# Two chained transformer blocks on one core: one merged norm stage with the narrow products in it, attention with stationary values, decay rows by transposes

## The reference

```python
# first block: bidirectional gated delta net, 8 heads of 128, chunks; then a 16-expert MoE
gcum = jnp.cumsum(g, axis=-1)
diff = gcum[..., :, None] - gcum[..., None, :]
decay = jnp.where(incl, jnp.exp(jnp.where(incl, diff, 0.0)), 0.0)
...
return rmsnorm(h, final_g)
# second block, on that result x
hx = rms_norm(x, norm1) * (1 + sc1) + sh1          # 1024 latent rows
hc = rms_norm(ctx, norm1) * (1 + csc1) + csh1      # 256 context rows
zx, xbc_x, dt_x, qx, kx, vx = split_projection(hx @ w_in)   # widths 512, 1024, 16, 512, 128, 128
zc, xbc_c, dt_c, qc, kc, vc = split_projection(hc @ w_in)
... # depthwise convolution and silu on xbc, two state-space scans, times silu(z), norm
# windowed attention: 8 query heads, 2 key/value heads, head width 64
p = softmax_with_sink(jnp.concatenate([s_loc, s_ctx], axis=-1), sink)
o = einsum('bnhgqk,bnkhd->bnqhgd', p_loc, vw) + einsum('bnhgqk,bkhd->bnqhgd', p_ctx, v_ctx)
x = x + g1 * (concatenate([ssd_x, attn_x]) @ w_out)
# then a 32-expert MoE and a last norm
```

## Time and profile before

| | us |
|---|---|
| median of 3 runs | 4789.37 (4787.4 to 4795.4) |
| profiled execution: time | 4788.9 |
| profiled execution: span of the profile | 4786.9 |
| PE busy in the span | 4181.8 (87%) |
| DVE, ACT, POOL busy | 1566.7, 795.1, 403.6 |
| norm stages n3 and n4, to the first projection product | 2809.5 to 2926.8 |
| projection, main part | 2926.8 to 3173.3 |
| projection, narrow products | 3173.3 to 3248.3 |
| attention, first product to last copy | 3432.0 to 3637.6 |

### The profile page before, as it was taken

One profiled execution on the slowest core, in us unless ns is written; L12 is line 12 of the kernel. 1 busy time (PEld: TensorE's weight loads), 2 busy tenths in 40 slices (PEclk: granted clock), 3 DMA queues, 4 the chain that ended last, 5 costly groups with the idle time before them and its releaser, 6 DMA issues. The chain is left out here.

```text
span 4786.9 us, 43588 instructions
## 1 busy us (share of the span) xinstructions
PE 4181.8 (87%) x15052; PEld 2319.5 (48%) x15052; DVE 1566.7 (33%) x3340; ACT 795.1 (17%) x1787; POOL 403.6 (8%) x388
## 2 busy tenths in 40 slices
PE   6699999997959999999999945997798789999962
PEld 3466666665414444444444423456675344444421
DVE  4577777775350000000000034416743400000003
ACT  2233333332110000000000001101252110001001
POOL 0111111110000000000000000004300000000001
PEclk8899999998969999999999967998799899999986
DMA  6211111111469888888888822100102189999855
GB/s 260 50 33 36 35 38 35 39 26 30 179 269 359 307 308 309 307 310 305 309 309 311 311 93 92 28 9 5 68 1 110 51 319 335 334 335 335 305 206 215
DMA packets 434795, 875.48 MB, mean 183 GB/s; under 512 B 88722, under 2 KB 132578, under 8 KB 428506
## 3 DMA queue, kind: packets, MB, share of 16 engines
q1 hardware_dynamic: 408361, 785.27, 46.6%
q0 software_dynamic: 20320, 74.06, 4.6%
q10 hardware_dynamic: 5968, 14.29, 0.8%
HBM read 801.14 MB, written 72.43 MB: 182 GB/s over the span
## 5 line engine op out<-in xcount | busy, mean ns | idle before, releaser
L1823 PE MATMUL moe_gbank<-moe_ring,moe_xT 128*128 128x512 f32 x1536 | 679.7, 596 | 3.8 <-ACTq L1879 3.8
L1841 PE MATMUL moe_acc<-moe_ring,moe_hidT 128*128 128x512 f32 x1536 | 675.1, 592 | 1.8 <-DVEq L1938 1.1
L1823 PE MATMUL moe_ubank<-moe_ring,moe_xT 128*128 128x512 f32 x1536 | 675.1, 592 | 0.0
L1913 DVE TENSOR_TENSOR moe_hid<-moe_sg,moe_ubank 128x512 f32<-128x512 f32 x96 | 66.0, 688 | 1631.8 <-PE moe_ubank L1823 1631.8
L921 PE MATMUL gdn_pbank<-mix_xT,gdn_w 128*128 128x512 f32 (+1 forms) x1280 | 540.8, 556 | 2.6 <-PEq L815 2.6
L1823 PEld LDWEIGHTS moe_gbank<-moe_ring,moe_xT 128*128 128x128 f32 x1536 | 293.4, 191 | 373.6 <-issue 370.3
L1841 PEld LDWEIGHTS moe_acc<-moe_ring,moe_hidT 128*128 128x128 f32 x1536 | 288.2, 190 | 347.1 <-issue 347.1
L1823 PEld LDWEIGHTS moe_ubank<-moe_ring,moe_xT 128*128 128x128 f32 x1536 | 284.5, 190 | 322.4 <-issue 322.4
L1884 ACT ACTIVATE moe_sg<-moe_gbank 128x512 f32<-128x512 f32 x96 | 57.3, 597 | 1547.4 <-PE moe_gbank L1823 1547.4
L921 PEld LDWEIGHTS gdn_pbank<-mix_xT,gdn_w 128*128 128x128 f32 x1280 | 230.2, 195 | 161.2 <-issue 152.4
L2059 PE MATMUL proj_abank<-mix_yT,proj_wq 128*128 128x512 f32 x416 | 180.8, 592 | 0.6 <-PE proj_abank L2059 0.6
(11 more groups left out here) (520 smaller groups left out, 4940.0 us busy)
## 6 DMA issues: line engine op xcount, KB each, us to landing
moe_ring<-in_moe_w_gate SPq DMA_DIRECT2D x64, 2048.0 KB, 7.9
moe_ring<-in_moe_w_up SPq DMA_DIRECT2D x64, 2048.0 KB, 7.8
moe_ring<-in_moe_w_down SPq DMA_DIRECT2D x64, 2048.0 KB, 7.8
moe_ring<-in_w_gate SPq DMA_DIRECT2D x32, 2048.0 KB, 8.7
moe_ring<-in_w_up SPq DMA_DIRECT2D x32, 2048.0 KB, 9.4
moe_ring<-in_w_down SPq DMA_DIRECT2D x32, 2048.0 KB, 9.8
front_wt<-in_w_mod SPq DMA_DIRECT2D x24, 1024.0 KB, 13.9
route_wt<-in_w_ada SPq DMA_DIRECT2D x24, 1024.0 KB, 16.0
```

The lines of the kernel that those rows point to most:

```text
L1823: last = nc.tensor.matmul(bank[:], xT[:, k, :], w[:, k * 512:(k + 1) * 512], start=(k == 0), stop=(k == KD - 1))
L1841: last = nc.tensor.matmul(acc[j][:], hidT[:, k, :], w[:, k * D + j * 512:k * D + (j + 1) * 512], start=(f == 0 and k == 0), stop=(f == NF ...
L1913: nc.vector.tensor_tensor(hid[:], sg[:], ubank[:], ALU.mult).then_inc(u_free, 1)
```

## The change

1. `delta_net`: the decay rows' calls become transposes of the same broadcast column.
2. `n3` and `n4` become one stage `norms_and_narrow`. Its parameters for both kinds of rows are loaded ahead, ACT takes over the sums of squares, and the z, dt and v products are made there, one token tile behind the transposes. It uses four x buffers and three y buffers. The first two weight tiles of the projection and the convolution weights are loaded at its end.
3. `project` loses the narrow products, their loads and the first two weight loads; silu of z is one instruction at its end.
4. `attention`: the values are stationary (64 columns) and the probabilities move, two heads at once (256 columns). Even heads go to PSUM partitions 0 to 63, odd ones to 64 to 127 of the same bank. The reciprocals are spread over partitions by four small products, DVE copies them out and multiplies straight into `yT2`. `at`, its transposes and their copies are gone.

```diff
 # delta_net, fill
-  last = nc.tensor.matmul(b[:, q * P:(q + 1) * P], tab[:, n, C_, u:u + 1].broadcast_to([P, P]), ident, start=True, stop=True)
+  last = nc.tensor.transpose(b[:, q * P:(q + 1) * P], tab[:, n, C_, u:u + 1].broadcast_to([P, P]), ident)
 # attention, PE
-  for g in range(QPK):
-      for c in kt:
-          last = nc.tensor.matmul(obank[u % 2][:, g * HD:(g + 1) * HD], pT[:, c, g, :], vtok[:, vt, kv * HD:(kv + 1) * HD], ...)
-  last.then_inc(o_full, 1)
-  ... (after the last unit: transposes of at, per token tile)
+  for c in kt:
+      for odd in range(2):
+          last = nc.tensor.matmul(obank[u % 2][odd * HD:(odd + 1) * HD, 0:2 * P], vtok[:, vt, kv * HD:(kv + 1) * HD], pT[:, c, odd::2, :], ...)
+  last.then_inc(o_full, 1)
+  pe.wait_ge(rec_ready, u + 1)
+  for g in range(QPK):
+      j, odd = divmod(g, 2)
+      last = nc.tensor.matmul(obank[u % 2][odd * HD:(odd + 1) * HD, (2 + j) * P:(3 + j) * P], stats[u % RING][:, REC_, g:g + 1].broadcast_to([P, HD]), ident, start=True, stop=True)
+  last.then_inc(r_full, 1)
 # attention, DVE: for each unit reciprocals(u), maxima(u + 2), divide(u)
-  nc.vector.tensor_tensor(at[...], obank[...], stat[:, REC_, :]..., ALU.mult).then_inc(o_free, 1)
+  nc.vector.tensor_copy(rb[...], bank[:, 2 * P:4 * P])
+  dve.drain()
+  nc.vector.tensor_tensor(yT2[:, 4 + 2 * kv:6 + 2 * kv, n * P:(n + 1) * P], bank[:, 0:2 * P]..., rb[:], ALU.mult).then_inc(o_free, 1)
 # project
-  for t in range(NA): ... z and dt/v products, their copies out, wz and wv loads
-  nc.scalar.activation(z[:, t, :], b[:], ACT.Silu).then_inc(a_free, 1)
+  nc.scalar.activation(z[...all eight tiles...], z[...], ACT.Silu)
```

More of the change, by code:

```diff
@@ L1949, in softplus_steps, with project @@
     nc.vector.tensor_scalar(x, x, 0.0, None, ALU.max)
-def project(nc, xT, w_in, conv_w, conv_b, cst, ident, BC, Btok, xs, z, dtr, qT, kT, vtok):
+def project(nc, xT, w_in, cst, ident, BC, Btok, xs, z, qT, kT, cwr, wq):
     XT = 8
@@ L1959, in project @@
     with Stage(nc, "proj") as st:
-        cwr = st.sb("cwr", [(CONV + 1) * XT, P])
         cw = st.sb("cw", [P, (CONV + 1) * XT])
-        wq = [st.sb(f"wq{i}", [P, KD, P]) for i in range(2)]
-        wz = st.sb("wz", [P, KD, 512])
-        wv = st.sb("wv", [P, KD, 2 * SH + KVH * HD])
         raw = [st.sb(f"raw{i}", [P, PADTOK]) for i in range(2)]
@@ L2069, in _ @@
                         rotate(i - 1)
-                for t in range(NA):
-                    if t >= NC_T:
-                        b = a_bank()
-                        for k in range(KD):
-                            last = nc.tensor.matmul(b[:], x_cols(k, t * P, P), wz[:, k, :], start=(k == 0), stop=(k == KD - 1))
-                        last.then_inc(a_full, 1)
-                    b = d_bank()
-                    for k in range(KD):
-                        last = nc.tensor.matmul(b[:, 0:2 * SH + P], x_cols(k, t * P, P), wv[:, k, :], start=(k == 0), stop=(k == KD - 1))
-                    last.then_inc(d_full, 1)
-                    if t == NA - 1:
-                        rotate(XT + QPK)
+                rotate(XT + QPK)
             @block.scalar
@@ L2122, in _ @@
                         act.sem_inc(rot_ready, 1)
-                for t in range(NT):
-                    b = take()
-                    nc.scalar.activation(z[:, t, :], b[:], ACT.Silu).then_inc(a_free, 1)
+                nc.scalar.activation(z[:].rearrange("p t c -> p (t c)"), z[:].rearrange("p t c -> p (t c)"), ACT.Silu)
             @block.vector
@@ L2181, in _ @@
                     rotate(i)
-                for t in range(NA):
-                    b = take()
-                    nc.vector.tensor_copy(dtr[:, t, :], b[:, 0:2 * SH])
-                    nc.vector.tensor_copy(vtok[:, t, :], b[:, 2 * SH:2 * SH + P])
-                    dve.drain()
-                    dve.sem_inc(d_free, 1)
                 rotate(XT + QPK)
@@ L2605, in _ @@
                         context(u + 2)
-                for t in range(NT):
-                    act.wait_ge(t_full, ntr + 1)
-                    nc.scalar.activation(yT2[:, 4:8, t * P:(t + 1) * P], tbank[ntr % 2][:].rearrange("p (k n) -> p k n", k=4), ACT.Copy).then_inc(t_free, 1)
-                    ntr += 1
             @block.vector
@@ L2635, in maxima, with reciprocals @@
                     nc.vector.tensor_scalar(stat[:, NEG_, :], stat[:, LMAX_, :], -1.0, None, ALU.mult).then_inc(m_ready, 1)
-                def divide(u):
-                    n, kv = units[u]
+                def reciprocals(u):
                     stat = stats[u % RING]
@@ L2653, in _ @@
                 for u in range(len(units)):
+                    reciprocals(u)
                     if u + 2 < len(units):
```

342 lines of the change are left out of this document (202 added, 140 removed).

## The result

The changed kernel takes 4678.09 us (median of 4 runs, 4670.21 to 4678.51); the kernel before, on the same chip, 4792.39 (4787.4 to 4796.46). The ratio is 0.9753, 95% interval 0.9741 to 0.9765. In a later set the same pair gave 4676.88 and 4793.63, ratio 0.9756 (0.9743 to 0.9769). The prediction said 4683. The profiled executions, on which its sum rests, have spans of 4786.9 and 4676.5: -110.4, where the sum said -106.5.

A forecast was written before the change was run, and what follows sets the result against it. PE, busy 87% of the span, was taken to bound the kernel, with DVE pacing n3 and n4. Delta -10, merged norm stage with `project` -67.5 and attention -29 sum to -106.5 us, giving 4683, range 4664 to 4723.

The forecast's parts named there:

- Delta, booked -10: Delta stage: decay rows by transposes save 1.4 us a head over seven heads, -10 us, bounds 0 and -18.4.
- Start of the new stage, booked +8: Merged norm stage: loads, first tiles, stream and change of stage make `project` start at 125 instead of 117.3 us, +8.
- Narrow products, booked -75: `project`: the narrow products leave it for the merged stage, -75 us.
- Project's first sixteen products, booked -1.5: Start of `project`: PE comes from a full stream, so half the slow-clock loss of 6.2 against 3.45 us returns, -1.5.
- Key tile's rotation, booked +1: `project`: the key tile's rotation, formerly covered by narrow products, now waits for ACT's copy, +1 us.
- Attention, booked -29: Attention: twelve units save 1.65 us, four about 1.1, total -24; the removed end gives -4.7; sum -29 us.
- The rival of halves one after the other: Attention: column halves don't overlap, a unit pays 4.3 + 0.9 + 0.3 against 4.5; +11 instead of -29, 4723 us; chance 0.11.
- 0.2 that I took off for another break of the stream: Attention unit: one more break of PE's stream, from a new shape and a reciprocals wait, cuts the 1.85 us saving to 1.65.
- the prediction's estimate of 0.17 by that rule: Attention unit: one more change of tiling mode drains TensorE and costs some 0.17 us, leaving 1.68 of 1.85 saved.
- The rule of the Trainium skill: Attention: it would give the rival that weight loads are paid in series, +6.1 us a unit, 4805 us; chance 0.02.
- The handing over between engines: Merged stage: engines waiting for each other set the pace, 12.5 us a tile, adding 22, 4705 us; chance 0.10.

The follow-up runs named there:

- `norm_later`: The changed kernel with DVE's four small key-norm instructions moved behind r of the scan's step 1; 4670.28 us, ratio 0.9742 to the kernel before.
- `one_half`: The changed kernel with every attention value product written to the lower column half (output differs); 4638.29 us, not comparable as the last experts' stage ran fewer products.
- `halves_in_turn`: The changed kernel with attention's two value loops exchanged, all even heads' products before all odd ones; 4691.04 us, ratio 0.9785 to the kernel before.
- `after`: The changed kernel itself, without further edits; 4678.09 us, ratio 0.9753 to the kernel before.
- `warm`: The changed kernel with 24 further unused transposes at the end of PE's list in the merged stage; 4677.82 us, ratio 0.9763 to the kernel before.

## Why the prediction was right, step by step

The forecast, 4683 in 4664 to 4723, was met at 4678, and by its own mechanisms. That it was met within 5 us is in part luck: terms that were off by 1 to 5 us went both ways.

- *Delta, booked -10.* Measured -10.0 by the means of 3 and 8 executions. DVE does take back a part of PE's 18.4 us, as said: a wait for r of 0.65 us a head where I had 0.9, so a head without a dip is 1.6 us shorter and not 1.4. What I didn't see is that DVE's list ahead of r also holds four small norm instructions, 0.7 us from the first of them to r, which can be moved behind it without loss (`norm_later`).
- *Start of the new stage, booked +8.* It was +3.5. DVE started on the parameters at 16.55 us (I took 17), z at 41.9 (44), the stream took 76.1 (76), and `project` came 2.8 us behind it (4.5). The first z and the change of stage are the misses, 2.1 and 1.7 us. In the second I had counted z's last copy behind PE's last product; it ended before it (2919.3 against 2920.6), and only DVE's copies ran on, for 0.4 us.
- *Narrow products, booked -75.* They are gone from `project`: the full 75.0 of the earlier trace rows.
- *Project's first sixteen products, booked -1.5.* (I took 6.2 us for them before; start to start the rows say 6.4.) In this execution nothing came back: from the first of them to the key tile's rotation 247.1 us instead of 246.5. In five other executions all 3 us did, in four 1.2 us; the mean over the eleven, 1.7, is near what I booked, but by luck: the reason I gave, PE coming from a full stream, was there in all eleven and didn't decide.
- *Key tile's rotation, booked +1.* It was +2.2 (from its first product to the next stage's first transfer 8.5 us instead of 6.3). Mis-sized: I had counted ACT's copy, but the rotation of the last query, too, had been covered by narrow products, and DVE now has both in front of it, twelve instructions from 3169.97 to 3177.93.
- *Attention, booked -29.* It was -30.3 in the profiled pair, a unit of 10.92 for 11.0, and more against the old attention's other executions. The rival of halves one after the other had the right price for the values: +2.15 a unit measured in `one_half`, 4.3 - 2.2 = 2.1 in my terms; that the reciprocals would then cost 0.9 singly was not tried. Of the 0.2 that I took off for another break of the stream 0.13 was spent: saved were 1.72 of 1.85, and the break is the 0.14 us between the reciprocals' products and the transposes. The Trainium skill ("TensorEngine Tiling (Array Packing)", Key Properties) says that changing the tiling mode drains TensorE; the trace agrees, and the prediction's estimate of 0.17 by that rule was close.
- *The rule of the Trainium skill* ("TensorE: Matmul & The Clock Gate", Part 3) by which weight loads overlap a running matmul only if the row groups differ is not what the rows show: in `one_half`, where all value products use the same rows and the same half of the columns, each load takes 0.14 us and the products still start 0.216 apart.
- *Not booked:* -3.3 us in the tables and the state-space scan, -2.7 of it in the scan, where PE is busy 120.3 instead of 123.0 us with the same 720 instructions. As said above it repeats in all eleven executions with the new norm stage and `project`, and in none of the three with the old ones, though no instruction of the scan was changed. Why stays open; the scan's mean granted clock doesn't settle it (0.81, 0.81 and 0.83 in the three, 0.80 to 0.82 in the eleven). Small rests: +1.0 ahead of the norm stage apart from the delta stage, and -1.2 behind attention, where the next stage's first product comes 5.1 us behind that stage's first transfer instead of 6.7.

The handing over between engines, the rival with 0.10, can be seen in the first tiles only (waits of 4.43 and 0.66 us above). That four x buffers and one tile of lead kept it out of the stream is argued from the lists; no run had fewer.

## What to carry to other kernels

Where two stages run one after the other and each is held by another engine, merging them can be worth the shorter one's time nearly in full (here 71.5 of 75.0 us), where every wait in the busiest engine's list is met by work one tile ahead; what is left to gain is then in the order of the first tiles, and it was 9 of the 42 us here. When an edit shortens one engine's share of a loop that two engines pace, look at everything that the other has queued in front of the item that is waited for: moving small work behind it gave some 4 us in the heads, over a third of what the edit gave (6.6 in the time, good to about 5). Compare stage by stage over several executions: the first pair was off by 2 us in the delta stage and by some 5 in attention, where stretches at the lower clock differed.

## What the runs showed of the hardware

- Two products into different column halves start 0.006 us apart and each half keeps its 0.216 us from start to start; three instructions in the list between them don't prevent it (`halves_in_turn`, where two of L2632 start ahead of three of L2627 that precede them in the list).
- Going from products with 64 active columns to transposes with 128 costs 0.14 us (starts 0.20 and 0.17 apart instead of 0.11 and 0.12).
- The granted clock behind an idle gap of 2.6 us was full (1.00) in one execution and mostly at the lower level (0.53) in another with the same list ahead of it (3.72 and 6.69 us for the same sixteen instructions of 256 columns), and lower for a part (5.4 us) in four executions whose lists differed a little.
- Stretches at the lower level fall at different places in each execution: the new attention took 174.2 us at a mean granted clock of 0.98 and 178.9 at 0.95, the old one 205.0 at 0.97 and 215.4 at 0.91.
- The change of stage took 2.1 to 2.2 us from the end of the engine that ended last to the next stage's first PE instruction (`after`, `warm`).
